# First projection panel of a two-block transformer kernel in one-tile units, with other first loads

## The reference

```python
for l in range(DEPTH):                       # first block, DEPTH = 2
    h = rms_norm(x, attn_norm_g[l])
    proj = h @ w_in[l]
    c_q, c_kv, k_rope, gq, gk, gv, pool_in, gate_logits = split_columns(proj, IN_SIZES)
    o_mla = mla_branch(c_q, c_kv, k_rope, ...)
    o_gqa = gqa_branch(gq, gk, gv, gqa_q_head_g[l], gqa_k_head_g[l], cos_g, sin_g)
    o_pool = pool_branch(pool_in, pool_w[l], pool_scale[l])
    ...
    x = x + merged @ w_out[l]
    hf = rms_norm(x, ffn_norm_g[l])
    ...
return second_block(x, ...)
```

## Time and profile before

| | |
|---|---|
| median of 3 runs | 1474.56 us (1474.46 to 1474.73) |
| the profiled execution's own time | 1474.63 us |
| its span, first to last instruction | 1472.8 us |
| PE busy | 1464.2 us, 99% |
| PEld, DVE, ACT, POOL busy | 1236.0, 1101.3, 883.6, 56.1 us |
| DMA moved | 256.75 MB, 174 GB/s on the mean |
| granted PE clock | 1.00 in all of the stretches read |

### The profile page before, as it was taken

One profiled execution on the slowest core, in us unless ns is written; L12 is line 12 of the kernel. 1 busy time (PEld: TensorE's weight loads), 2 busy tenths in 40 slices (PEclk: granted clock), 3 DMA queues, 4 the chain that ended last, 5 costly groups with the idle time before them and its releaser, 6 DMA issues.

```text
span 1472.8 us, 20097 instructions
## 1 busy us (share of the span) xinstructions
PE 1464.2 (99%) x7790; PEld 1236.0 (84%) x7790; DVE 1101.3 (75%) x1666; ACT 883.6 (60%) x1340; POOL 56.1 (4%) x69
## 2 busy tenths in 40 slices
PE   9999999999999999999999999999999999999998
PEld 7878888888897778888888877888888888888887
DVE  7898779996578878799956667875467567887446
ACT  6555657775447565677744576664456555666435
POOL 0110000000021000000000001000000000100001
PEclk9999999999999999999999999999999999999999
DMA  8643546666555435465555533656546534556562
GB/s 300 205 134 115 165 142 207 192 193 198 173 166 183 129 115 176 168 188 198 191 190 201 174 99 117 232 187 193 194 158 234 170 121 142 170 196 195 190 189 83
DMA packets 74015, 256.75 MB, mean 174 GB/s; under 512 B 8640, under 2 KB 9920, under 8 KB 73920
## 3 DMA queue, kind: packets, MB, share of 16 engines
q1 hardware_dynamic: 73776, 255.46, 53.1%
q10 hardware_dynamic: 144, 0.00, 0.0%
HBM read 254.38 MB, written 1.05 MB: 173 GB/s over the span
## 4 chain that ended last, share of the span: by engine, by line
PE 90%; DVE 5%; ACT 2%; DMA 1%; POOL 1%; issue 0%; SPq 0%; DVEq 0%; ACTq 0%; POOLq 0%
PE psum L1300 19%; PE psum L1327 17%; PE psum L1331 17%; PE psum L1329 17%; PE psum L1306 10%; PE psum L1256 4%; DVE w_low L2228 2%; DMA w_raw<-in_weights 1%; PE psum L1471 1%; PE psum L1561 1%; PE psum L1503 1%; ACT w_high L1716 1%; PE psum L1611 1%; PE psum L1643 1%; DVE scratch L2209 0%
## 5 line engine op out<-in xcount | busy, mean ns | idle before, releaser
L2228 DVE TENSOR_TENSOR w_low<-w_raw,w_high 128x1024 fp32r<-128x1024 f32 (+2 forms) x482 | 574.4, 1199 | 209.6 <-ACT w_high L1716 208.8
L1716 ACT ACTIVATE w_high<-w_raw 128x1024 fp32r<-128x1024 f32 (+2 forms) x482 | 498.5, 1039 | 252.1 <-PE psum L1331 217.5
L1300 PE MATMUL psum<-x_parts,w_high 128*128 128x512 f32 x992 | 248.8, 393 | 0.0
L1300 PEld LDWEIGHTS psum<-x_parts,w_high 128*128 128x128 f32 x992 | 178.6, 189 | 32.1
L1327 PE MATMUL psum<-w_high,x_parts 128*128 128x512 f32 (+2 forms) x432 | 169.6, 393 | 0.7 <-DVE w_low L2228 0.7
L1329 PE MATMUL psum<-w_low,x_parts 128*128 128x512 f32 (+2 forms) x432 | 163.9, 379 | 0.0
L1331 PE MATMUL psum<-w_high,x_parts 128*128 128x512 f32 (+2 forms) x432 | 163.8, 379 | 0.0
L1306 PEld LDWEIGHTS psum<-x_parts,w_low 128*128 128x128 f32 x992 | 135.3, 190 | 9.7
L1306 PE MATMUL psum<-x_parts,w_low 128*128 128x256 f32 x992 | 138.3, 282 | 0.0
L1327 PE MATMUL psum<-w_high,ff_high 128*128 128x512 f32 x256 | 99.8, 390 | 0.0
L1329 PE MATMUL psum<-w_low,ff_high 128*128 128x512 f32 x256 | 99.6, 389 | 0.0
(11 more groups left out here) (287 smaller groups left out, 2321.2 us busy)
## 6 DMA issues: line engine op xcount, KB each, us to landing
w_raw<-in_weights SPq DMA_DIRECT2D x450, 512.0 KB, 3.7
w_raw<-in_weights SPq DMA_DIRECT2D x16, 384.0 KB, 3.0
w_raw<-in_weights SPq DMA_DIRECT2D x7, 416.0 KB, 3.8
rows<-in_second_rows SPq DMA_DIRECT2D x4, 512.0 KB, 5.0
w_raw<-in_weights SPq DMA_DIRECT2D x6, 256.0 KB, 2.7
scratch<-in_x_turned SPq DMA_DIRECT2D x4, 256.0 KB, 5.0
residual<-in_x SPq DMA_DIRECT2D x2, 512.0 KB, 7.0
dil_masks<-in_consts SPq DMA_DIRECT2D x1, 768.0 KB, 6.1
```

The source lines that it names most:

```text
L1300: eng.matmul(acc[:, f * PANEL:(f + 1) * PANEL], wh[:, j, f * P:(f + 1) * P], parts[:, k, :, :].rearrange("p s n -> p (s n)"), start=k == 0 ...
L1716: act(self.unit_view(self.wh, u), raw, ACT.Copy).then_inc(sem("w_high"), 1)
L2228: tt(self.unit_view(self.wl, u), raw, self.unit_view(self.wh, u), ALU.subtract).then_inc(sem("w_low"), 1)
```

## The change

Panel 0 is cut into eight units of one tile each; the loads after the first bring two of them at a time, and the eighth unit has a load of its own. The gain columns are packed behind the first piece of tokens, so that one DMA brings both, and the waits of ScalarE, VectorE and GpSimd on a load of their own are gone. ScalarE issues the first unit's weights, and SyncE leaves them out. Each later tile's `arrive` stands behind a unit of its own; the squares come behind units 8 and 9, the token rows behind loads 5 and 6, the constants behind load 7, `load_rows` behind unit 12, `row` 13, `tables` 14, `take_c` comes two units after the end of panel 0, its norm three and four after, `lora` eight.

```diff
@@ weight_units
-            first = [0, 1, 2, 3] if not units and not own else []
+            first = list(range(kts)) if not units and not own else []
...
-        if n == 3:
+        if n in (2, 4, 6):
@@ Plan.arrive
-        def later():
-            add("arrive", 4)
-            add("arrive", 5)
-            self.prefetch(0, 4)
-            add("arrive", 6)
-            add("arrive", 7)
+        def later(k):
+            add("arrive", k)
+            self.prefetch(0, k)
...
-        self.after(2, later)
-        self.after(3, lambda: (add("square", g, 0), add("mean", g), self.prefetch(0, 6), add("square", g, 1),
-                               add("rstd", g)))
-        self.after(4, lambda: (add("constants"), add("diag", g)))
+        for k in range(4, DK):
+            self.after(k - 3, lambda k=k: later(k))
+        self.after(8, lambda: (add("square", g, 0), add("mean", g)))
+        self.after(9, lambda: (add("square", g, 1), add("rstd", g)))
+        self.after(10, lambda: (add("constants"), add("diag", g)))
@@ Plan.mixing
-            self.after(5, lambda: add("load_rows", l))
+            self.after(12, lambda: add("load_rows", l))
-        self.after(9, lambda: add("row", g))
+        self.after(9 if l else 13, lambda: add("row", g))
-        self.after(9, lambda: add("tables", l))
+        self.after(9 if l else 14, lambda: add("tables", l))
...
+            if panel == 0 and not l:
+                self.after(2, lambda: add("take_c", l))
+                self.after(3, lambda: add("c_norm_a", l))
+                self.after(4, lambda: add("c_norm_b", l))
+                self.after(8, lora)
+                return
@@ memory
-        self.arriving = by_tile(self.scr[:, 0:DK * SEQ])
+        piece = 2 * SEQ
+        self.arriving = [by_tile(self.scr[:, (j or 4) * piece:(j or 4) * piece + piece]) for j in range(4)]
+        self.first_piece = self.scr[:, 4 * piece:5 * piece + DK]
+        self.first_gain = self.first_piece[:, piece:]
@@ sync
+                if n == 0:
+                    continue
...
-                elif 4 <= n <= 5:
+                elif 5 <= n <= 6:
...
-                elif n == 6:
+                elif n == 7:
...
-                load_arriving(0)
+                eng.dma_start(self.first_piece, dram["x_turned"][:, 0:2 * SEQ + DK]).then_inc(sem("x_arrived0"), 16)
@@ scalar
-        eng.dma_start(self.cols[:, 0:DK], self.dram["first_cols"][0][:, 0:DK]).then_inc(sem("first_loaded"), 16)
+        at_0, size_0 = self.loads[0]
+        eng.dma_start(self.raw[0][:, 0:size_0], self.dram["weights"][at_0:at_0 + P * size_0].rearrange("(p n) -> p n", p=P)
+                      ).then_inc(sem("w_loaded0"), 16)
         eng.preload_act_table_set("exp_and_others")
-        q.wait_ge(sem("first_loaded"), 16)
```

More of the change, by code:

```diff
@@ L1075, in load_arriving @@
         def load_arriving(j):
-            eng.dma_start(self.arriving[:, 2 * j:2 * j + 2, :],
-                          dram["x_turned"][:, 2 * j * SEQ:(2 * j + 2) * SEQ].rearrange("p (k s) -> p k s", s=SEQ)
+            at = DK + 2 * j * SEQ
+            eng.dma_start(self.arriving[j], dram["x_turned"][:, at:at + 2 * SEQ].rearrange("p (k s) -> p k s", s=SEQ)
                           ).then_inc(sem(f"x_arrived{j}"), 16)
@@ L1093, in sync @@
                     load_arriving(n)
-                elif 4 <= n <= 5:
-                    c = slice((n - 4) * PANEL, (n - 3) * PANEL)
-                    eng.dma_start(self.x[:, :, c], src[:, :, c]).then_inc(sem(f"x_loaded{n - 4}"), 16)
-                elif n == 6:
+                elif 5 <= n <= 6:
+                    c = slice((n - 5) * PANEL, (n - 4) * PANEL)
+                    eng.dma_start(self.x[:, :, c], src[:, :, c]).then_inc(sem(f"x_loaded{n - 5}"), 16)
+                elif n == 7:
                     eng.dma_start(self.consts, dram["consts"][:, 0:N_HELD]).then_inc(sem("consts_loaded"), 16)
@@ L1723, in scalar @@
                 q.wait_ge(sem(f"x_arrived{k // 2}"), 16)
-                act(self.features[STAGE_MIX[0]][0][:, k, :], self.arriving[:, k, :], ACT.Copy,
-                    scale=self.gain(STAGE_MIX[0])[:, k:k + 1]).then_inc(sem("arrived_high"), 1)
+                q.wait_ge(sem("x_arrived0"), 16)
+                act(self.features[STAGE_MIX[0]][0][:, k, :], self.arriving[k // 2][:, k % 2, :], ACT.Copy,
+                    scale=self.first_gain[:, k:k + 1]).then_inc(sem("arrived_high"), 1)
             elif kind == "turn":
@@ L2237, in vector @@
                 q.wait_ge(sem("arrived_high"), k + 1)
-                stt(low[:, k, :], self.arriving[:, k, :], self.gain(STAGE_MIX[0])[:, k:k + 1], high[:, k, :], ALU.mult,
+                stt(low[:, k, :], self.arriving[k // 2][:, k % 2, :], self.first_gain[:, k:k + 1], high[:, k, :], ALU.mult,
                     ALU.subtract).then_inc(sem("arrived_low"), 1)
```

4 lines of the change are left out of this document (2 added, 2 removed).

## The result

| | before | after |
|---|---|---|
| median, lowest to highest of 12 runs | 1474.69 us, 1474.11 to 1475.40 | 1478.28 us, 1476.53 to 1479.36 |
| the profiled execution's own time, span | 1474.63, 1472.8 us | 1477.88, 1476.1 us |
| ratio of the times | | 1.0023 (95% interval 1.0015 to 1.0030) |

What follows compares the result with a forecast made beforehand. PE was taken to bound the kernel (99% of the span): 0.93 us gained at 15.8 us, given back in a wait of about 1.5 us at 60, net +0.4, so 1475.0 us; range 1473.6 to 1476.0.

Steps and rivals of the forecast that it cites:

- What bounds: Whole kernel: PE is busy 1464.2 us, 99% of the span, so the change reaches the time only where PE waits.
- The shift s: VectorE's gates step near 60 us, which PE waits for: comes 0.4 us later than in the kernel before.
- unit 12 lands: Load of the first unit of the third panel (key and value heads): lands at 21.3 us, 0.35 us less than before.
- The landings: Weight loads after the start: 1 MB and more always asked for ahead, so units are ready before PE wants them; no loss.
- The upper bound that I kept for the queue: Loads before unit 12: one more piece of 256 KB ahead would cost 0.6 us more, s = +1.0; not taken.
- GpSimd's steps: GpSimd's step for the norm vector: 0.71 us, as in the kernel before, within 1.75 us from VectorE's second square.
- The gain column and the queue: Start of the kernel: gain with the tokens, first weights on ScalarE's queue and three removed waits, booked at 0.
- The hole closes: PE's hole before the fifth unit, near 12 us: closes, putting PE 0.93 us ahead from 15.8 us on.
- The rival: The change doesn't close the hole: third token piece lands after 9.7 us; 0 us by itself; no separate chance given.
- slower by 1 to 2.9 us: Norm vector later than 27.6 us holds ScalarE, VectorE, then PE, each us costing one: 1475.6 to 1477.5 us; chance 0.17.
- slower by more: Slower beyond 0.2%, through a second missed step in the first layer; chance 0.03.
- The gain stays: VectorE's chain to 60 us is faster than walked, so PE keeps its lead: 1473.4 to 1474.6 us; chance 0.28.

Runs made afterwards that it cites:

- e1: The changed kernel with its loads paired as in the kernel before (units 2+3, 4+5, 6+7 together, the rest alone): 1475.36 us.
- e7: The changed kernel with only the token rows and constants back behind the loads they had before (token rows behind loads 4 and 5): 1474.77 us.
- e10: The kernel before with only the gain column in the first token piece and the first weights on ScalarE's queue: 1474.08 us.
- e11: The changed kernel itself run once more, nothing altered: 1478.41 us.
- e5: The changed kernel with both the old pairing of loads and the old order of squares, constants, compressed vectors and rows: 1473.65 us.
- e2: The kernel before with only the change's late order of steps and later token rows, keeping its own units, loads and gain columns: 1476.67 us.
- e6: On top of e1, the scaling of the compressed vectors one unit later, so two low parts stand beside GpSimd's small steps: 1475.22 us.
- e4: The changed kernel with the constants and token diagonals one unit earlier, right behind the reciprocal root of the tokens: 1477.28 us.

## Why the prediction was wrong, step by step

**What bounds: right.** PE holds the time, and a hole closed ahead of 60 us is given back at VectorE's chain. e1 and e7 show it: panel 1 starts at 15.69 and 15.72, over 1.0 us ahead of before (16.75), PE then waits 1.04 and 0.94 for the copy, and its transposes start at 60.30 and 60.24 (60.27 before). In all traces span less the start of PE's transposes is 1412.4 to 1412.7 us wherever the clock stayed up after the wait there, so that start alone sets the rest.

**The shift s: mechanism right, size wrong**, 3.26 us where I had 0.4 (0.37 unrounded). By my own terms:

| term | predicted | measured | difference |
|---|---|---|---|
| unit 12 lands | 21.3 | 23.03 | +1.73 |
| from there to the norm vector | 5.65 | 6.64 | +0.99 |
| norm vector to the end of the heads' sum | 16.15 | 17.18 | +1.03 |
| end of the sum to the copy of the key heads | 16.66, as before | 15.80 | -0.86 |
| sum | | | +2.89 |

0.37 + 2.89 = 3.26.

- **The landings.** The step that failed is "yet 1 MB and more is still asked for ahead of each: no loss". I counted how much was asked for, and not when: load 5 waited for a pair until 8.92 us, and the token rows behind it, moved there by the change, could not fill the gap. I had also taken the later token rows as a pure gain for the weights. e7 shows that without this move the loads come in time: unit 12 at 20.63, 0.67 ahead even of my 21.3. The upper bound that I kept for the queue, 0.6 us, was short by a factor of three.
- **GpSimd's steps.** I took 0.71 us from the row of before for the norm vector's step. It took 1.62, since VectorE's low part had begun 0.16 us ahead of it; and the first step for the compressed vectors took 1.10, where it had taken 0.19 in the kernel before. Those are the +0.99 and most of the +1.03. The -0.86 is the same effect the other way round: GpSimd's step of 20 columns took 3.53 us instead of 4.38. In the kernel before it began behind the second of three low parts of weights:

```profile
44.02 4.38 POOL L2808 TENSOR_TENSOR stat<-stat,minus_half 128x20 f32<-128x20 f32 x1
...
42.65 3.52 DVE L2228 TENSOR_TENSOR w_low<-w_raw,w_high 128x1024 fp32r<-128x1024 f32 x3
```

In the changed kernel the low parts of the compressed vectors, whose first operand is in PSUM, had begun ahead of it (47.89). All 13 traces divide that way: 4.38 us in the six with a low part of weights there, 3.53 in the seven with those of the compressed vectors. A duration read in one order was carried into another. Where no such thing happened, my terms hold: in e7 from the second square (24.61) to the norm vector (26.36) 1.75 us, the number predicted.
- **The gain column and the queue, booked at 0: wrong, as far as e10 shows it.** e10 is 0.9 us faster than before by the medians, 0.5 us by its trace. The failing sentence is "an earlier issue moves no bytes", drawn from a DMA share of 1.02. The share was full, the rate was not: 368 GB/s before and 403 in e10 between 7 and 9 us at shares of 1.03 and 1.02. The Trainium skill, "DMA: Bandwidth & Descriptors", section "Issuing engines are not separate DMA queues", which I took to bound the gain at one issue's 0.4 us, does not explain it: unit 8 came 1.0 us sooner. e10 doesn't refute the page either, since it also does away with the single small load of gains (4 KB); what part of the gain that is was not tried apart.
- **The hole closes: only by chance.** It did not in the first profile (1.14 us of wait ahead of panel 1), it did in e11. The 0.93 us that I had for it are 0.95 by my own rows (16.75 less 15.80); nothing hangs on that. The rival said that this costs nothing by itself, and so it was.

**The rivals.** By mechanism it is "slower by 1 to 2.9 us": the norm vector later than 27.6 us. Its place, its queue on ScalarE and, within 0.2 us, its price of one us for one us are borne out (29.67 is 2.72 after my 26.95, and s is 2.89 above mine); its chance, 0.17, was too small. But 3.6 us lie above its upper end. By time it is "slower by more", to which I gave 0.03 and for which I named a second missed step in the first layer; GpSimd's step behind VectorE's low part was one, beside the late loads. What I had against a slower kernel was a walk in which every term came from a row of another order. "The gain stays" fits e5, another kernel than the changed one.

**Beyond the trace.** The medians lie 3.6 apart and the profiles 3.3; PE's clock, which fell after the wait in two of the profiles of this study, can account for the rest; that it does isn't shown. No term of mine had it.

## What to carry to other kernels

When a queue holds loads that wait for buffers, ask for each wait what stands behind it: a transfer that needs no buffer belongs ahead of the wait, and moving it one place back, behind a wait for a pair, cost this kernel 3.5 us, more than any hole that the change closed. Price a moved step by what will run beside it in the new order, and where a chain on another engine sets the start of the bounding one, shorten that chain first and count holes ahead of it as nothing. A wait of PE may be paid twice: here the granted clock was 0.50 for some us after waits of 2.07 and 2.38 us, which cost 0.8 to 0.9 us more, and stayed at 1.00 after waits of 1.85 (e2) and 3.05 us.

## What the runs showed of the hardware

**GpSimd's small steps wait for VectorE's operation with two operands in SBUF.** The pairs below are GpSimd's start and end, and the end of VectorE's low part of 1024 columns that had begun ahead of it:

| kernel, step | alone | GpSimd | VectorE's low part |
|---|---|---|---|
| changed, first of the mean | 0.19 | 26.13 to 27.15 | 25.88 to 27.10 |
| changed, norm vector | 0.71 | 28.05 to 29.67 | 27.89 to 29.11 |
| e6, norm vector | 0.71 | 25.80 to 27.42 | 25.63 to 26.85 |
| e10, first of the compressed | 0.19 | 26.94 to 28.14 | 26.87 to 28.10 |
| e6, second of the compressed | 0.19 | 33.99 to 35.05 | second of two, to 35.00 |
| e5, third of the compressed (4 columns) | 1.01 | 27.59 to 29.45 | 27.33 to 28.58 |
| before, norm of the heads (20 columns) | 3.53 | 44.02 to 48.40 | second of three, 43.78 to 45.00 |

"Alone" is the duration of the same step in traces where no low part of weights was running when it began. The step of 0.19 us ends 0.04 to 0.05 after VectorE's; the step of 0.71 us ends 0.56 to 0.57 after it, that of 1.01 us 0.87 and that of 3.53 us 3.40. So in each case what is left behind VectorE's end is the step's own time less 0.13 to 0.15 us. In e1 and e7 the same step began ahead of the low part (25.79 against 25.95, and 25.65 against 26.69) and took 0.71. In e11 it began only 0.03 us ahead (27.57 against 27.60) and took 0.71 too. VectorE was not held in either order: its low part took 1.22 to 1.24 us in all of these, and in no trace is one of 1024 columns longer than 1.26. The Trainium skill, "SBUF — State Buffer", section "Who interferes with whom", says that a VectorE instruction with two SBUF inputs contends with a GpSimd instruction that reads SBUF, and that the order of issue decides who blocks. The rows agree with the first, and with the second as far as GpSimd waits when it comes second; that VectorE waits when GpSimd comes first no run here shows. Had I used it in the prediction, two of its terms would have been 0.9 us longer and the step of 20 columns 0.85 shorter.

**A full DMA share is not a full rate.** At shares of 1.02 to 1.05 the rates read here go from 362 GB/s (before, 4.4 to 10.1 us) to 413 (e7, 13 to 15 us).

**The end of PE's warm-up moves from run to run.** Its six passes took 4.25 us in the first profile of the changed kernel and 5.49 in e11, the same kernel, 5.49 before, and 4.4 to 4.6 in e1, e2 and e4, and e2 has the start of the kernel before. The second real matmul came at 6.53 in that first profile and at 7.07 in e11. So the 0.4 us by which the first profile was ahead of the 6.95 of before can't be put down to the change.
